# The norm of a transformer trunk on VectorE and ScalarE alone, and the two chunks behind it multiplied tile by tile in turn

## What is computed

```python
for l in range(2):
    h = modulate(rms_norm(x, g_mix[l]), mod[:, :, 0], mod[:, :, 1])      # first norm; hc the same from ctx
    y, yc = token_mixer(h, hc, w_in[l], ...)      # retention, MLA, GQA on h @ w_in, gates, w_out
    x = x + mod[:, :, 2] * y
    h2 = modulate(rms_norm(x, g_ffn[l]), mod[:, :, 3], mod[:, :, 4])     # second norm
    x = x + mod[:, :, 5] * swiglu(h2, w_ffn_in[l], w_ffn_out[l])
    ...                                           # xc the same in the first layer only
return rms_norm(x, g_final)
# rms_norm(x, g) = x * rsqrt(mean(x*x) + eps) * g;  modulate(x, shift, scale) = x * (1 + scale) + shift
```

## Time and profile before

| | us |
|---|---|
| median of 3 runs | 3745.88 (3745.24 to 3748.95) |
| the profiled execution | 3743.77 |
| its span, first to last instruction | 3741.9 |
| TensorE busy with matmuls | 3305.7 (88%) |
| VectorE busy | 1550.6 (41%) |
| ScalarE busy | 1281.4 (34%) |
| GpSimd busy | 477.3 (13%) |
| mean granted clock of TensorE | 0.938 |

### The profile page before, as it was taken

One profiled execution on the slowest core, in us unless ns is written; L12 is line 12 of the kernel. 1 busy time (PEld: TensorE's weight loads), 2 busy tenths in 40 slices (PEclk: granted clock), 3 DMA queues, 4 the chain that ended last, 5 costly groups with the idle time before them and its releaser, 6 DMA issues.

```text
span 3741.9 us, 50235 instructions
## 1 busy us (share of the span) xinstructions
PE 3305.7 (88%) x18696; PEld 2786.6 (74%) x18696; DVE 1550.6 (41%) x1997; ACT 1281.4 (34%) x1778; POOL 477.3 (13%) x340
## 2 busy tenths in 40 slices
PE   6788897999999988799999967988798999879998
PEld 4678776888888876588888746777677777758886
DVE  4455423544334433422222245653455344453334
ACT  3344332444333332221211223443344333433222
POOL 2011100111000000300000130220011001021001
PEclk8888898999999999899999978999899999989999
DMA  4111141111321123124233231212111321223332
GB/s 159 55 43 56 38 124 40 61 56 60 115 65 62 53 91 128 51 63 133 73 95 107 96 124 54 68 59 84 56 58 61 99 64 62 82 93 100 93 99 95
DMA packets 91434, 297.11 MB, mean 79 GB/s; under 512 B 10320, under 2 KB 16592, under 8 KB 91344
## 3 DMA queue, kind: packets, MB, share of 16 engines
q1 hardware_dynamic: 55872, 202.40, 17.1%
q10 hardware_dynamic: 35472, 93.49, 7.6%
HBM read 274.88 MB, written 20.97 MB: 79 GB/s over the span
## 4 chain that ended last, share of the span: by engine, by line
PE 40%; issue 9%; DVE 6%; ACT 3%; DMA 3%; POOL 1%; ACTq 0%; DVEq 0%; POOLq 0%
PE ps L1278 37%; DMA mraw<-in_wmod 2%; DVE prob L1001 1%; PE ps L1366 1%; DVE mx L838 1%; PE ps L1344 1%; POOL ptl L1260 1%; ACT pth L437 1%; DVE tmp L983 0%; DVE tmp L817 0%; ACT wh L384 0%; DVE wl L807 0%; DVE ptl L856 0%; DVE xz L1165 0%; DVE tmp L877 0%
## 5 line engine op out<-in xcount | busy, mean ns | idle before, releaser
L1278 PE MATMUL ps<-hh,wh 128*128 128x512 f32 x2768 | 835.0, 362 | 123.0 <-POOL hl L1242 64.0
L1278 PE MATMUL ps<-hl,wh 128*128 128x512 f32 x2768 | 823.1, 358 | 0.0
L1278 PE MATMUL ps<-hh,wl 128*128 128x512 f32 x2768 | 820.5, 357 | 0.0
L807 DVE TENSOR_TENSOR wl<-raw,wh 128x1024 fp32r<-128x1024 f32 x364 | 481.9, 1324 | 696.8 <-ACT wh L384 669.3
L1278 PEld LDWEIGHTS ps<-hh,wh 128*128 128x128 f32 x2768 | 457.7, 192 | 223.9 <-issue 59.0
L1278 PEld LDWEIGHTS ps<-hh,wl 128*128 128x128 f32 x2768 | 458.5, 192 | 78.5
L1278 PEld LDWEIGHTS ps<-hl,wh 128*128 128x128 f32 x2768 | 459.9, 193 | 73.6
L384 ACT ACTIVATE wh<-raw 128x1024 fp32r<-128x1024 f32 x364 | 382.8, 1052 | 245.9 <-PE ps L1278 202.6
L1278 PE MATMUL ps<-yh,wh 128*128 128x512 f32 (+1 forms) x1296 | 410.2, 371 | 37.4 <-DVE yl L1132 17.1
L1278 PE MATMUL ps<-yl,wh 128*128 128x512 f32 (+1 forms) x1296 | 397.8, 361 | 0.0
L1278 PE MATMUL ps<-yh,wl 128*128 128x512 f32 (+1 forms) x1296 | 397.4, 361 | 0.0
(11 more groups left out here) (176 smaller groups left out, 3729.3 us busy)
## 6 DMA issues: line engine op xcount, KB each, us to landing
raw<-in_stream SPq DMA_DIRECT2D x364, 512.0 KB, 3.6
mraw<-in_wmod ACTq DMA_DIRECT2D x80, 512.0 KB, 3.7
gspill<-prob ACTq DMA_DIRECT2D x24, 384.0 KB, 2.3
tmp<-gspill ACTq DMA_DIRECT2D x24, 384.0 KB, 3.1
early<-in_wmod SPq DMA_DIRECT2D x16, 512.0 KB, 15.0
dec<-in_dec ACTq DMA_DIRECT2D x8, 768.0 KB, 4.2
gspill<-side ACTq DMA_DIRECT2D x24, 256.0 KB, 2.2
tmp<-gspill ACTq DMA_DIRECT2D x24, 256.0 KB, 2.7
```

The costliest lines, as they stand in the source:

```text
L807: dve.tensor_tensor(wl[:, s, :], raw[:, s, :], wh[:, s, :].bitcast(F32), ALU.subtract).then_inc(sem("w_lo"), 1)
L1278: ins = pe.matmul(out, lhs[w], rhs[x](cols), start=start and n == 0, stop=stop and n == 2)
```

## The change

The norm of a tile becomes three operations. VectorE makes `tmp = (xz * gm) * rstd` in one SCALAR_TENSOR_TENSOR, with one instruction per piece since `gm` differs for latent and context tokens; ScalarE makes `hh = tmp + shift`, rounded; VectorE makes `hl = (tmp + shift) - hh` in a second SCALAR_TENSOR_TENSOR. GpSimd's part and the count `n_full` are gone. VectorE waits with tile t for its own low half of tile t - 2 (`n_lo`).

The first two chunks behind a norm are multiplied together, tile by tile in turn (`project_pair`): tile 0 for slot 0, tile 0 for slot 1, tile 1 for slot 0, and so on. It takes both weight slots at the start, so the split of chunk 1 moves ahead of the norm: into `root` before Sqrt on ScalarE, and before the reciprocal on VectorE. In `mla_in` and in the first turn of the first `ffn` phase that split is left out where it was; that turn is written out ahead of the loop. The other calls of `project` behind a norm no longer wait for `n_lo`.

```diff
@@ scalar
             def root(at, n, nt):
 
+                if at.v("chunk") < NCHUNK:
+                    split(at, 1)
                 act.wait_ge(sem("sq_used"), at.v("sq_used", n))
...
                             ins = act.activation(hh[:, t, r0:r1], tmp[:, t % 2, r0:r1], ACT.Identity,
-                                                 bias=mods[:, layer, 3 * gi * KT + t, u:u + 1],
-                                                 scale=gm[:, gi, t, u:u + 1])
+                                                 bias=mods[:, layer, 3 * gi * KT + t, u:u + 1])
...
                         for k in range(RKT):
-                            split(at, 2 * j + k + 1)
+                            if j + k:
+                                split(at, 2 * j + k + 1)
...
                 elif kind == "ffn":
-                    with act.Fori(0, turns) as i:
+                    def turn(i, paired=False):
                         t = At(ph, i)
                         for k in range(2):
-                            split(t, 2 * k + 1)
+                            if not paired or k:
+                                split(t, 2 * k + 1)
...
+                    if ph["paired"]:
+                        turn(0, paired=True)
+                    with act.Fori(1 if ph["paired"] else 0, turns) as i:
+                        turn(i)
@@ vector
                 elif kind in ("squares", "summed"):
+                    if at.v("chunk") < NCHUNK:
+                        split(at, 1)
                     dve.wait_ge(sem("n_std"), at.v("n_std", 1))
...
                             if t >= 2:
-                                dve.wait_ge(sem("n_hi"), at.v("n_hi", t - 1))
-                                dve.wait_ge(sem("n_full"), at.v("n_full", t - 1))
-                            dve.tensor_tensor(tmp[:, t % 2, 0:nt], xz[:, t, 0:nt], tmp[:, 2, 0:nt],
-                                              ALU.mult).then_inc(sem("n_t1"), 1)
+                                dve.wait_ge(sem("n_lo"), at.v("n_lo", t - 1))
+                            for u, (r0, r1) in enumerate(ranges(nt)):
+                                ins = dve.scalar_tensor_tensor(out=tmp[:, t % 2, r0:r1], in0=xz[:, t, r0:r1],
+                                                               scalar=gm[:, gi, t, u:u + 1], in1=tmp[:, 2, r0:r1],
+                                                               op0=ALU.mult, op1=ALU.mult)
+                            ins.then_inc(sem("n_t1"), 1)
                         m = t - 1
                         if m >= 0:
-                            if m >= 2:
-                                dve.wait_ge(sem("n_lo"), at.v("n_lo", m - 1))
-                            dve.wait_ge(sem("n_t1"), at.v("n_t1", m + 1))
+                            dve.wait_ge(sem("n_hi"), at.v("n_hi", m + 1))
                             for u, (r0, r1) in enumerate(ranges(nt)):
-                                ins = dve.tensor_scalar(prob[:, m % 2, r0:r1], tmp[:, m % 2, r0:r1],
-                                                        gm[:, gi, m, u:u + 1],
-                                                        mods[:, layer, 3 * gi * KT + m, u:u + 1], ALU.mult, ALU.add)
-                            ins.then_inc(sem("n_full"), 1)
+                                ins = dve.scalar_tensor_tensor(
+                                    out=hl[:, m, r0:r1], in0=tmp[:, m % 2, r0:r1],
+                                    scalar=mods[:, layer, 3 * gi * KT + m, u:u + 1],
+                                    in1=hh[:, m, r0:r1].bitcast(F32), op0=ALU.add, op1=ALU.subtract)
+                            ins.then_inc(sem("n_lo"), 1)
@@ gpsimd
-                elif kind == "norm":
-                    for t in range(KT):
-                        pool.wait_ge(sem("n_hi"), at.v("n_hi", t + 1))
-                        pool.wait_ge(sem("n_full"), at.v("n_full", t + 1))
-                        pool.tensor_tensor(hl[:, t, 0:nt], prob[:, t % 2, 0:nt], hh[:, t, 0:nt].bitcast(F32),
-                                           ALU.subtract).then_inc(sem("n_lo"), 1)
@@ tensor
+            def project_pair(at, nt):
+
+                for slot in range(2):
+                    if at.v(f"free{slot}") > 0:
+                        pe.wait_ge(sem(f"free{slot}"), at.v(f"free{slot}"))
+                pe.wait_ge(sem("w_lo"), at.v("chunk", 2))
+                for kt in range(KT):
+                    pe.wait_ge(sem("n_lo"), at.v("n_lo", kt + 1 - KT))
+                    for slot in range(2):
+                        s = at.slot(slot)
+                        outs = [(pair(slot)[:, r0:r1], (r0, r1)) for r0, r1 in ranges(nt)]
+                        ins = three(outs, [w[:, s, whole(kt)] for w in (wh, wl)],
+                                    [lambda c, x=x: x(kt, c) for x in H], kt == 0, kt == KT - 1)
+                        if kt == KT - 1:
+                            ins.then_inc(sem("product"), 1)
...
                     for j, nt_j in enumerate((TOK if layer < DEPTH - 1 else LAT, TOK)):
-                        for k in range(RKT):
-                            project(at, 2 * j + k, k, j, H, KT, nt_j, whole, late=normed(at))
+                        if j == 0:
+                            project_pair(at, nt_j)
+                        for k in range(RKT if j else 0):
+                            project(at, 2 * j + k, k, j, H, KT, nt_j, whole)
...
                         for k in range(2):
-                            for j in range(2):
-                                project(t, 2 * k + j, j, k, H, KT, nt, whole, late=normed(at))
+                            if paired and k == 0:
+                                project_pair(t, nt)
+                            else:
+                                for j in range(2):
+                                    project(t, 2 * k + j, j, k, H, KT, nt, whole)
```

More of the change, by code:

```diff
@@ L131, in plan @@
         squares = {"sq": KT, "sq_used": KT, "n_std": 1, "n_rstd": 1}
-        norm = {"n_t1": KT, "n_hi": KT, "n_full": KT, "n_lo": KT}
+        norm = {"n_t1": KT, "n_hi": KT, "n_lo": KT}
         if layer == 0:
@@ L176, in plan @@
             phase("ffn", layer, n // 2, {"chunk": 4, "free0": 2, "free1": 2, "f_hi": 2, "f_lo": 2},
-                  nt=nt)
+                  nt=nt, paired=g == 0)
             nmod = 2 - 2 * layer
@@ L1180, in _, with turn @@
                 elif kind == "ffn":
-                    with dve.Fori(0, turns) as i:
+                    def turn(i, paired=False):
                         t = At(ph, i)
                         for k in range(2):
-                            split(t, 2 * k + 1)
+                            if not paired or k:
+                                split(t, 2 * k + 1)
                             split(t, 2 * k + 2)
@@ L1190, in _ @@
                                               ALU.mult).then_inc(sem("free1"), 1)
+                    if ph["paired"]:
+                        turn(0, paired=True)
+                    with dve.Fori(1 if ph["paired"] else 0, turns) as i:
+                        turn(i)
                 elif kind == "final":
@@ L1301, in _ @@
             whole = lambda kt: slice(kt * P, (kt + 1) * P)
-            def normed(at):
-                return {kt: ("n_lo", at.v("n_lo", kt + 1 - KT)) for kt in range(KT)}
             def stats(at, src, slots, nt, k):
@@ L1624, in _, with turn @@
                 elif kind == "ffn":
-                    with pe.Fori(0, turns) as i:
+                    def turn(i, paired=False):
                         t = At(ph, i)
                         for k in range(2):
-                            for j in range(2):
-                                project(t, 2 * k + j, j, k, H, KT, nt, whole, late=normed(at))
+                            if paired and k == 0:
[3 more added lines that the diff above has]
+                                    project(t, 2 * k + j, j, k, H, KT, nt, whole)
+                    if ph["paired"]:
+                        turn(0, paired=True)
+                    with pe.Fori(1 if ph["paired"] else 0, turns) as i:
+                        turn(i)
 def halves(dim):
```

## The result

| | before | changed kernel |
|---|---|---|
| median of 4 runs each, us | 3745.56 (3736.33 to 3748.95) | 3694.55 (3688.20 to 3701.38) |
| ratio, 95% interval | | 0.9863 (0.9844 to 0.9881) |
| span of the profiled execution, us | 3741.9 | 3686.4 |
| mean granted clock | 0.938 | 0.949 |
| TensorE, VectorE, ScalarE, GpSimd busy, us | 3305.7, 1550.6, 1281.4, 477.3 | 3273.5, 1531.8, 1257.4, 403.7 |

The forecast was 3707.4 us, with 3696 to 3720 as its range: 38.5 us of gain where 51.0 came. The direction was right, the size too small, and the time lies 1.5 us outside the range.

A forecast was written before the change was run, and what follows sets the result against it. TensorE was taken to lose twice in four norms, waiting for GpSimd's low halves and running at the low clock. Gains of 13.4 + 11.2 + 14.5 + 6.2 = 45.3, less 6.8 for the clock, gave 38.5: 3707.4 us, range 3696 to 3720.

The forecast's parts named there:

- C: Layer 1's first norm and the chunks behind it: the norm's last tile sets the end, 14.5 us counted as gain.
- A: Layer 0's first norm and the chunks behind it: TensorE is the bound, sums start 13.4 us earlier.
- B: Layer 0's second norm and the chunks behind it: chunk 2 starts earlier, 11.2 us gained.
- D: Layer 1's second norm, of 512 columns, and the chunks behind it: 6.2 us gained.

The follow-up runs named there:

- p1: Changed kernel plus a useless GpSimd addition of 448 columns beside every tile of the norm; 3713.13 us (one execution).
- n2: Kernel before with only the paired chunks and the early split of chunk 1, on the old norm; 3717.93 us, ratio 0.9924.
- n1: Kernel before with only the norm in three operations, chunks in their old order; 3707.59 us, ratio 0.9898.
- o0: Changed kernel with the turns undone: all eight tiles of chunk 0, then all of chunk 1; 3701.55 us, ratio 0.9899.
- w1: Changed kernel plus useless TensorE products ahead of each norm's first low half, to start the pair at full clock; 3685.41 us, ratio 0.9842.
- w2: Changed kernel plus w1's useless products, with turns on the first six tiles only (four in D), then chunk by chunk; 3678.57 us, ratio 0.9823.

## What to carry to other kernels

Where an engine waits piece by piece for a producer, give it the work of the next task on the same pieces: the gain is that work, and, where at the lower clock it then fills the producer's pace, as in C here, an earlier rise of the clock too. Then look at what the removed tail had covered, and leave just enough of it: four to six tiles of eight in turns gave stretches 5.7 and 5.3 us shorter than all eight. When a loop's first turn is written out, ask for each table load on which side of the wait it will now stand; and before a range is made, measure how far the untouched part of the kernel differs between two executions.

## What the runs showed of the hardware

- ScalarE's table load of 1.28 us can hide ahead of a wait: in straight code it was done 4.15 us before its operation's data came; in the loop it came after the wait.
- The two-input operation on VectorE is stretched from 479 to 1069 ns for 256 columns beside GpSimd's addition of 1.37 us, and ends 0.3 us after that has ended. The Trainium skill, "SBUF — State Buffer", section "SBUF: two separate sides", gives this as sharing of one pair of ports; p1 agrees.
- TensorE's clock at its higher level stayed up through repeated waits: 0.2 to 0.6 us in 2.24 (C of the changed kernel), 1.1 to 1.7 us in 3.34 (C of n2). In A of n1 it fell among waits of 0.9 us in 2.24. At its lower level it did not rise while waits of 0.5 to 0.6 us came with every tile (C of o0 and n1, 13.4 us), and rose 5.6 and 5.8 us after the last of them.
- After 2.6 to 2.9 idle us the clock was still up in w1 (B, C, D) and fell within the next 1.1 us; after 1.35 and 1.69 idle us in w2 (B, C) it stayed up.
- Even products that wait for nothing run differently from one execution to the next. The 32 small products of the modulation ahead of norm A, of before and of the changed kernel:

```profile
39.16 5.64 PE L1464 MATMUL ps<-sel,prob 128*128 128x2 f32 x32 [0.69 <-ACT prob L568]
```

```profile
39.32 3.73 PE L1488 MATMUL ps<-sel,prob 128*128 128x2 f32 x32 [0.69 <-ACT prob L570]
```

The mean granted clock was 0.63 over the first and 1.00 over the second. The change doesn't touch these products, and norm A began between 43.25 and 46.9 us over the profiles.
